# A stage of two unrolled halves written as hardware loops of two turns on three engines

## The reference, cut to what matters

```python
hn = rmsnorm(x, lp['norm_mix'])
q, k, v, f_logit, xr, gr = jnp.split(hn @ lp['w_in'], SPLIT_IDX, axis=-1)
...
xc, conv_new = causal_dwconv(xr, conv_buf, lp['rnn_conv_w'], lp['rnn_conv_b'])
gate_a = jnp.einsum('btnc,ncd->btnd', xb, lp['w_rg_a']).reshape(b, t, D_RNN) + lp['b_rg_a']
gate_x = jnp.einsum('btnc,ncd->btnd', xb, lp['w_rg_x']).reshape(b, t, D_RNN) + lp['b_rg_x']
log_a = -RG_C * r * jax.nn.softplus(-lp['rg_lambda'].astype(jnp.float32))
u = jnp.sqrt(-jnp.expm1(2.0 * log_a)) * (i * xc.astype(jnp.float32))
h = linear_recurrence(a, u, h0.astype(jnp.float32))
y = h * jax.nn.gelu(gr.astype(jnp.float32))
```

## Time and profile before

| | |
|---|---|
| median of three executions | 3233.12 us (3231.55 to 3233.87) |
| the profiled execution's own time | 3231.55 us |
| its span, first to last instruction | 3229.8 us |
| TensorE busy | 2987.9 us, 93% |
| VectorE, ScalarE, GpSimd busy | 1427.4, 755.3, 1205.8 us |
| granted TensorE clock, mean | 0.951 |
| the stage of the change | about 283 to 616 us |

### The profile page before, as it was taken

One profiled execution on the slowest core, in us unless ns is written; L12 is line 12 of the kernel. 1 busy time (PEld: TensorE's weight loads), 2 busy tenths in 40 slices (PEclk: granted clock), 3 DMA queues, 4 the chain that ended last, 5 costly groups with the idle time before them and its releaser, 6 DMA issues.

```text
span 3229.8 us, 46435 instructions
## 1 busy us (share of the span) xinstructions
PE 2987.9 (93%) x15701; PEld 2606.4 (81%) x15701; DVE 1427.4 (44%) x1921; ACT 755.3 (23%) x1533; POOL 1205.8 (37%) x577
## 2 busy tenths in 40 slices
PE   4999999777798989988999999999999998999998
PEld 4899999643454545547999999999999998999998
DVE  5312444377665666615135444554455543212221
ACT  7000333322232323334011000000000003443442
POOL 1111111137765666605773222222222223454443
PEclk9999999877888989998999999999999999999999
DMA  7212332447776787544451111111111114555553
GB/s 224 74 66 91 108 114 100 117 112 244 239 224 206 231 259 237 186 128 162 136 184 60 45 43 52 52 41 45 46 52 46 47 53 167 197 181 175 186 196 108
DMA packets 249057, 422.72 MB, mean 131 GB/s; under 512 B 44693, under 2 KB 152418, under 8 KB 244370
## 3 DMA queue, kind: packets, MB, share of 16 engines
q1 hardware_dynamic: 167986, 322.58, 31.6%
q10 hardware_dynamic: 80616, 97.07, 9.0%
q0 software_dynamic: 288, 1.05, 0.1%
HBM read 337.21 MB, written 83.46 MB: 130 GB/s over the span
## 4 chain that ended last, share of the span: by engine, by line
PE 75%; SPq 5%; DVE 5%; issue 4%; DMA 4%; POOL 3%; ACT 3%; ACTq 0%; DVEq 0%; POOLq 0%
PE PS L2559 34%; PE PS L2224 14%; PE PS L2647 4%; PE PS L2649 4%; PE PS L2443 4%; PE PS L2648 4%; SPq L603 3%; SPq L596 2%; PE PS L2467 1%; DMA Vpg<-in_cache_v 1%; PE PS L2427 1%; PE PS L2352 1%; PE PS L2429 1%; DVE YT L2173 1%; DVE MP L1825 1%
## 5 line engine op out<-in xcount | busy, mean ns | idle before, releaser
L2559 PE MATMUL PS<-MH,VS 128*128 128x416 f32 (+1 forms) x4000 | 1080.4, 351 | 3.8 <-issue 2.2
L2559 PEld LDWEIGHTS PS<-MH,VS 128*128 128x128 f32 x4000 | 749.4, 188 | 14.1 <-issue 5.5
L2559 PE MATMUL PS<-ML,VS 128*128 128x416 f32 (+1 forms) x2000 | 699.8, 350 | 0.0
L2559 PEld LDWEIGHTS PS<-ML,VS 128*128 128x128 f32 x2000 | 376.0, 188 | 2.6 <-issue 0.8
L1071 POOL TENSOR_TENSOR DL<-DR,DH 128x1408 fp32r<-128x1408 f32 x80 | 258.5, 3231 | 286.3 <-ACT DH L1496 286.2
L924 POOL TENSOR_TENSOR prod<-Kpg,qb 128x1024 f32<-128x1024 f32 x118 | 279.4, 2367 | 167.5 <-DMA Kpg<-in_cache_k 81.1
L2443 PE MATMUL PS<-PT,VA 128*65 128x416 f32 (+16 forms) x816 | 335.2, 495 | 2.4 <-ACT PT L1359 1.8
L2647 PE MATMUL PS<-GH,DH 128*128 128x416 f32 (+1 forms) x880 | 315.0, 358 | 17.1 <-DVE GL L2155 8.9
L1000 POOL CAST VS<-VR 128x1024 fp32r<-128x1024 f32 x52 | 62.9, 1209 | 689.2 <-PE PS L2559 687.6
L2649 PE MATMUL PS<-GH,DL 128*128 128x416 f32 (+1 forms) x880 | 310.8, 353 | 0.0
L2648 PE MATMUL PS<-GL,DH 128*128 128x416 f32 (+1 forms) x880 | 309.2, 351 | 0.0
(11 more groups left out here) (286 smaller groups left out, 4313.4 us busy)
## 6 DMA issues: line engine op xcount, KB each, us to landing
Kpg<-in_cache_k SPq DMA_DIRECT2D x256, 256.0 KB, 4.6
Vpg<-in_cache_v SPq DMA_DIRECT2D x256, 256.0 KB, 4.2
DR<-in_w_down SPq DMA_DIRECT2D x80, 704.0 KB, 4.1
gT<-GO ACTq DMA_DIRECT2D x110, 208.0 KB, 1.9
VR<-in_w_up SPq DMA_DIRECT2D x44, 512.0 KB, 3.3
GRb<-gT SPq DMA_DIRECT2D x31, 416.0 KB, 5.0
WR<-in_w_stream SPq DMA_DIRECT2D x21, 512.0 KB, 3.4
GRa<-gT SPq DMA_DIRECT2D x24, 416.0 KB, 5.6
```

The lines of the kernel that those rows point to most:

```text
L2559: mm = e.matmul(PS[:, j, 0:full(j)], w[:, u, k], x[:, k, j * BW:j * BW + full(j)], start=(k == 0 and q == 0), stop=(k == KC - 1 and q == 2))
```

## The change

On TensorE, VectorE and ScalarE, the outer of the two Python loops over c becomes a hardware loop of two turns, whose body holds two c. VectorE's step counter gets the loop form, 26 steps a turn. No instruction that computes is added, removed or moved; SyncE's and GpSimd's programs are as they were.

```diff
@@ ScalarE
-            for i in range(2):
+            with e.Fori(0, 2) as i:
 
                 plan = []
                 count = [0, 0]
@@ VectorE
-            for i in range(2):
+            with e.Fori(0, 2) as i:
+                g_steps.start(i, 2 * 13)
                 for u in range(2):
                     c = 2 * i + u
                     n = 9 + 3 * c
...
                             e.tensor_tensor(x[:, 3:3 + TP], w[:], r[:], ALU.mult).then_inc(r_y, 1)
+                g_steps.stop(2)
```

## The result

The changed kernel takes 3253.63 us (median of 6, 3247.44 to 3260.01), the kernel before beside it 3228.91 us (6, 3222.64 to 3233.87): ratio 1.0079, interval 1.0062 to 1.0095, so some 25 us slower. I had forecast 3239, at most 3245, from a kernel before that stood at 3233.12 then: 6 us more, and 24.7 were measured. The profiled execution is one of the long ones: 3262.64 us, span 3260.9, 31.1 us over the span before.

A forecast was written before the change was run, and what follows sets the result against it. TensorE bounds the kernel, busy 93% of the span. Registers on ScalarE 1.8, registers elsewhere 0.8, TensorE's jump 0.4 and clock 3.1 sum to 6.1 us over the median 3233.12, giving 3239 us; range 3234 to 3245.

The forecast's parts named there:

- the jump on PE: TensorE's jump back between c=1 and c=2, behind L2334 with its queue empty: 0.4 us, other bound 4.9.
- I take it that 8 stay: TensorE's instruction memory holds 8 code blocks, one less than the 9 seen to fail at loop L2504.
- the body begins close behind a block's start and touches 7 blocks, not 8: TensorE's new loop body: about 1763 instructions, about 252 a block, so 7 blocks are just enough.
- half the code: One of three new things in the stage: its two code bodies become one; no separate term in the sum.
- Rival 1: The loop body does not stay in TensorE's instruction memory: the jump costs 4.8 us, total 3243.6; chance 0.25.
- ScalarE's registers: Computed DMA addresses and waits at the ends of c: 0.6 us a hole, three holes, 1.8 us (1.2 to 2.4).
- the holes: TensorE's idle times before L2334's transpose at each c's end, 1.50 us (1.73 at c=0/1); three of four count.
- The 1.50 us is ACT's queue: At each c's end ScalarE issues three DMAs (L1187, L1191, L1265) before copying the last block, so TensorE waits.
- TensorE's registers: Register work in TensorE's issue is hidden by its queue; only 0.2 us of it was priced, at the jump.
- The v part: ScalarE's four DMAs before the square root delay VectorE's chain; TensorE waits 0.2 us a c, 0.8 us (0 to 2.4).
- The clock: Longer holes at c=1/2 and 2/3 bring half clock behind them: 2 x 1.57 = 3.1 us (0 to 3.1).
- The jumps on VectorE and ScalarE: Their jumps back, ScalarE's priced as VectorE's 3.2 us, are covered: 0, at most 1 us.

The follow-up runs named there:

- bef_pad149: Kernel before plus 298 fulfilled waits (149 instructions) on TensorE ahead of attention, whose loop then begins 8 behind a block's start: 3229.75 us, ratio 1.0003.
- short_aligned: Changed kernel with 40 instructions left out of TensorE's loop body (now 1756) and 16 fulfilled waits ahead of the loop: 3230.77 us, ratio 1.0008.
- pad_stage32: Changed kernel plus 32 fulfilled waits (16 instructions) on TensorE ahead of the stage's loop: 3236.96 us, ratio 1.0027 to the kernel before.
- hole: Kernel before with ScalarE's copy of the last v block moved ahead of two DMAs (L1191, L1265) at each c's end: 3225.96 us, ratio 0.9986.
- dve_act: Changed kernel with TensorE written out again, loops only on VectorE and ScalarE: 3235.61 us, ratio 1.0019 to the kernel before.
- pad_att32: Changed kernel plus 32 fulfilled waits (16 instructions) on TensorE between the stage and the attention loop: 3241.39 us, ratio 1.0039 to the kernel before.
- after_att_unrolled: Changed kernel with the attention loop written out on TensorE, VectorE and ScalarE: 3233.42 us, ratio 1.0015 to the kernel before.
- short_unrolled: Kernel before, stage written out, with 2 of 24 matmuls a block left out in the q chunks: 3224.98 us, ratio 0.9993.
- bef_pad133: Kernel before plus 266 fulfilled waits (133 instructions) on TensorE ahead of attention, whose loop then begins 8 before a block's start: 3243.95 us, ratio 1.0039.

## Why the prediction was wrong

**The step that failed** is in the jump on PE: "I take it that 8 stay" with "the body begins close behind a block's start and touches 7 blocks, not 8". That 8 blocks are held was right (bef_pad149). The body was not where and what I took it for: 1796 instructions, more than 7 x 256 = 1792, so no alignment could have fitted it in 7, and it began 2 ahead of a block's start, so 9 blocks. I had read the count off the source: 412 matmuls for each c. The trace has 422, since the ten gate matmuls are two instructions each. So the body has 2 x 844 = 1688 matmuls and weight loads and 108 others, not 1648 and 115. The 860 matmuls of the earlier trace rows, 16 of them of the chunk before, could have told me: I counted 824 for that half. The starting point was on the wrong side of a block's start as well, and the choice hung on both. The term was 0.4 us with 4.9 as its other bound; it measured 9.00, since the bound came from a loop that pays one fetch at its jump, and this one pays two. The mechanism itself, that a body within the blocks held costs almost nothing, was right: short_aligned has it, at 0.26 us. That one fetch alone would have brought the 4.9 here is not shown: pad_stage32 stood 7.47.

**What was missing altogether.** I listed "half the code" as one of three new things and gave it no price outside the stage. It moved the attention loop from 115 behind a block's start to 8 before one: 0.39%, about 13 us, half of the loss. Rival 1 had the kind of thing right and gave 3243.6, 10.5 us more than before; with 9.00 in place of its 4.8 and these 13 it would have been 28 us, against 24.7 measured.

**ScalarE's registers**: 0.6 us a hole was too much; the holes grew by 0.07, 0.30 and 0.30 us, 0.67 in place of 1.8. The 0.13 us a DMA of the earlier trace rows did not carry over: the first of the three issues stands where it stood (L1187 0.66 us behind the copy's start before, 0.67 after), and the other two became shorter while they start later (L1191 0.50 to 0.45 us, L1265 0.44 to 0.35). "The 1.50 us is ACT's queue" was half right too: the run hole leaves 0.77 of it. **TensorE's registers**: I called them hidden by its queue, and for the matmuls inside a block they are. In c=3 the first L2224 behind the transpose came 0.1 us later than before and the gates another 0.2. **The v part**: 0.2 us a c forecast, 0.3 measured (VectorE's copy ends at 443.33+0.59=443.92 and the transposes start at 444.05, 0.04 idle). So c=1 and c=3, which have no jump, are 0.99 and 0.97 us longer. With the 0.28 us up to the end of c=0, and 12.68 - 9.00 - 2.9 = 0.8 for c=2, registers and v part make 3.0 us, and I had 2.6 for them: near, but by luck, as each share was off.

**The clock**: 3.1 us forecast, 2.9 measured, by another way and so by luck: behind the jump, none behind the hole at c=2/3. In dve_act it did come behind a hole of 1.69 us there. In pad_att32 and after_att_unrolled, whose stage is the changed kernel's, it came behind the same 1.80 us too, and the stretch behind the jump was 10.2 us in place of 13.7; c=1 to 3 took 262.5 and 262.3 us even so. The window behind the hole at c=2/3 in pad_att32:

```profile
546.00:549.40 3.40, 3.40 (x12) 3.27 (x11) 0.00 (x0) 0.27 (x1) 0.00 (x0) 0.51 0.63 224
```

**The jumps on VectorE and ScalarE** cost nothing on TensorE's path, as forecast. **Slower, within 0.2%, faster**: I gave slower 0.49, and my range ended 9 us too low, since its upper end was one fetch and no price at all for moved code.

The Trainium skill, "Runtime: NRT & Kernel Launch", section "Instruction fetch mechanics", gives TensorE 128 KiB of instruction memory, filled in blocks of 16 KiB that hold 256 instructions. The runs agree: the two stops are 2816 = 11 x 256 instructions apart, and in bef_pad149 a body of 8 blocks stays. The same section says that a taken branch stalls unless its target is in the current two-page window. On TensorE the runs differ: short_aligned jumps back over 7 blocks in 0.26 us, bef_pad149 over 8 in 0.40. The section's advice to prefer full unrolling is borne out for the attention loop, by 0.30%.

## What to carry to other kernels

Price a hardware loop on TensorE by its length in compiled instructions: where it touches up to 7 blocks of 256, the jump back was nearly free (0.26 us). Where it touched 8, the jump was free only if the ninth had not been fetched yet (0.40), and otherwise cost 4.5 to 5.0 us in attention and 7.5 in the stage. Where it touched 9, with its first instructions just ahead of a block's end, it cost 6.2 to 7.4 and 8.5 to 10.1. The half clock behind the stop comes on top. Any edit that changes the number of instructions moves all later loops of that engine, so compare later stages too, and see whether a few fulfilled waits ahead of a long loop undo it before blaming the edit. The attention loop, too long to stay loaded, was better written out (0.30%).

## What was unexpected

- The same idle time does not always bring the half clock. In short_unrolled a hole of 1.49 us at c=1/2 was followed by it, where the kernel before had 1.50 us and kept 1.00:

```profile
444.80:448.20 3.40, 3.38 (x11) 3.25 (x12) 0.00 (x0) 0.27 (x1) 0.28 (x1) 0.51 0.96 318
```

- 16 harmless instructions more or less on TensorE (bef_pad133 and bef_pad149, 32 waits) make 14 us.
- VectorE's branch at its jump in the stage was over in 0.3 us (I had priced it 3.2, as in attention), ScalarE's only after 3.3 us.
- The padding ahead of the stage's loop took its second stop away, yet the stage was no shorter (263.2 us against 262.5).
- Left open: why the first fetch begins 3.2 us after the branch in one kernel and 5.0 in another, why the ninth block comes at the end of one turn and not of another, and why bef_pad149 has one stop less and is not faster.
